# Turning the expert loop of a diffusion trunk layer: gate and up of slot s+1 ahead of down of slot s

## The reference

```python
gates = jnp.sum(jax.nn.one_hot(ids, N_EXPERTS, dtype=jnp.float32) * w_e[..., None], axis=-2).astype(h.dtype)
y = jnp.zeros_like(h)
for e in range(N_EXPERTS):
    hid = jax.nn.silu(h @ wg[e]) * (h @ wu[e])
    y = y + gates[..., e:e + 1] * (hid @ wd[e])
```

## Time and profile before

| | us |
|---|---|
| median of 3 runs | 1084.62 (1083.42 to 1086.98) |
| profiled execution | 1086.46 |
| its span, first to last instruction | 1084.7 |
| PE matmul busy | 900.0 (83%) |
| DVE busy | 718.8 (66%) |
| ACT busy | 415.1 (38%) |
| POOL busy | 392.1 (36%) |
| POOL down remainders (L621), 64 | 186.8 |
| DVE gate/up remainders (L1524), 62 | 156.8 |
| ACT rounding of gate/up (L1134), 64 | 119.5 |

### The profile page before, as it was taken

The page is one execution under the profiler, slowest core; times in us unless marked ns, Lnnn a source line. Parts: engine busy times, 40 slices in busy tenths (PEclk is TensorE's granted clock), DMA queues, the critical chain, the costliest instruction groups (busy, mean ns, idle before and its releaser), DMA issues.

```text
span 1084.7 us, 12383 instructions
## 1 busy us (share of the span) xinstructions
PE 900.0 (83%) x3689; PEld 632.3 (58%) x3690; DVE 718.8 (66%) x794; ACT 415.1 (38%) x520; POOL 392.1 (36%) x181
## 2 busy tenths in 40 slices
PE   6789999949798899992379998999999899988800
PEld 2354444414345478882358886888888677767700
DVE  2234778996883353446885778568646988888648
ACT  1333535325436221113242454435414556556212
POOL 1000735910000000003253647156341777766672
PEclk9989999969899999995589998999999888888955
DMA  8884405015205422316555748476452888887494
GB/s 318 292 330 135 176 20 193 0 39 187 105 0 203 184 78 112 117 78 255 188 190 212 279 168 317 159 271 238 158 223 86 317 317 309 325 311 268 168 358 190
DMA packets 96277, 213.48 MB, mean 197 GB/s; under 512 B 11007, under 2 KB 31613, under 8 KB 96253
## 3 DMA queue, kind: packets, MB, share of 16 engines
q1 hardware_dynamic: 85708, 174.37, 43.9%
q0 software_dynamic: 5904, 21.50, 5.5%
q10 hardware_dynamic: 4640, 17.30, 3.9%
HBM read 180.12 MB, written 33.03 MB: 197 GB/s over the span
## 4 chain that ended last, share of the span: by engine, by line
PE 51%; DVE 28%; issue 8%; DVEq 4%; DMA 3%; ACT 3%; POOL 2%; SPq 0%; ACTq 0%; POOLq 0%
PE bank L701 10%; DVE WP L1524 7%; PE bank L908 3%; PE bank L888 3%; PE bank L887 3%; PE bank L886 3%; PE bank L909 3%; PE bank L910 3%; PE bank L814 3%; PE bank L815 3%; PE bank L816 3%; DVE rkt L1538 2%; PE bank L745 2%; PE bank L683 2%; DVE U L1279 2%
## 5 line engine op out<-in xcount | busy, mean ns | idle before, releaser
L621 POOL TENSOR_TENSOR WP<-raw,WP 128x1024 fp32r<-128x1024 f32 x64 | 186.8, 2947 | 0.7 <-ACT WP L1138 0.5
L701 PE MATMUL bank<-hT,wring 128*128 128x512 f32 x384 | 169.3, 600 | 2.6 <-ACT hT L966 1.9
L1524 DVE TENSOR_TENSOR WP<-raw,WP 128x2048 fp32r<-128x2048 f32 x62 | 156.8, 2568 | 11.7 <-ACT WP L1134 8.3
L1134 ACT ACTIVATE WP<-raw 128x2048 fp32r<-128x2048 f32 x64 | 119.5, 1917 | 90.8 <-issue 84.9
L886 PE MATMUL bank<-WP,xp 128*128 128x512 f32 x368 | 144.1, 391 | 1.5 <-DVE xp L1561 1.5
L888 PE MATMUL bank<-WP,xp 128*128 128x512 f32 x368 | 143.8, 391 | 0.0
L887 PE MATMUL bank<-WP,xp 128*128 128x512 f32 x368 | 143.7, 391 | 0.0
L701 PEld LDWEIGHTS bank<-hT,wring 128*128 128x128 f32 x384 | 73.7, 193 | 93.5 <-issue 90.0
L617 POOL TENSOR_TENSOR held<-held 128x1 f32<-128x1 f32 x24 | 36.2, 1508 | 218.7 <-DVE idg L1553 210.8
L633 POOL TENSOR_TENSOR WP<-raw,WP 128x2048 fp32r<-128x2048 f32 x2 | 9.0, 4532 | 283.6 <-ACT WP L1134 283.6
L908 PE MATMUL bank<-WP,hp 128*128 128x512 f32 x184 | 83.2, 452 | 0.0
(11 more groups left out here) (278 smaller groups left out, 1503.6 us busy)
## 6 DMA issues: line engine op xcount, KB each, us to landing
raw<-in_expert_w_gate SPq DMA_DIRECT2D x64, 512.0 KB, 3.9
raw<-in_expert_w_up SPq DMA_DIRECT2D x64, 512.0 KB, 6.4
raw<-in_expert_w_down SPq DMA_DIRECT2D x64, 512.0 KB, 8.1
mring<-in_mod_w SPq DMA_DIRECT2D x20, 1024.0 KB, 5.3
expert_rows<-ysc ACTq DMA_DIRECT2D x23, 512.0 KB, 7.0
expert_rows<-g SPq DMA_DIRECT2D x16, 512.0 KB, 11.4
wring<-in_w_in SPq DMA_DIRECT2D x12, 512.0 KB, 6.0
mslot<-in_mod_w SPq DMA_DIRECT2D x4, 1024.0 KB, 14.9
```

Of the source, the lines that this page charges most:

```text
L621: pool.tensor_tensor(WP[:, j, 1, 2 * D:], raw[:, j, 2 * D:], WP[:, j, 0, 2 * D:].bitcast(F32), ALU.subtract).then_inc(s_lod[j], 1)
L701: mm = pe.matmul(o_, wring[:, n % 3, k, :], src, start=k == 0, stop=k == KD - 1)
L1134: A_(WP[:, j, 0, 0:2 * D], raw[:, j, 0:2 * D], ACT.Copy).then_inc(s_hgu, 1)
L1524: tt(WP[:, j, 1, 0:2 * D], raw[:, j, 0:2 * D], WP[:, j, 0, 0:2 * D].bitcast(F32), ALU.subtract).then_inc(s_logu[j], 1)
```

## The change

Only the expert loop and what surrounds it change.

- PE: the loop runs W-1 times. Turn q does gate and up of slot q+1, rows of q+2, numbers of q+3, down of q, hidden transposes of q+1. Gate and up of slot 0 with its transposes stand before the loop, down of the last slot after it. All four hidden transposes go to bank 7 and are released together.
- DVE: three gate/up remainders (not one) come ahead of the hidden product, the fourth after the row numbers; the scaling of slot q stands between that and the hidden remainder of q+1. Gate/up work goes by the flag of slot q+1. `gcol` has a column for every slot.
- ACT: three roundings of gate/up ahead of the tanh, then tanh, rows, the fourth rounding, the down roundings (by the flag of slot q), the hidden copy, the store of y.
- POOL: the gather is one slot further ahead; the down remainders go by the flag of q.
- SP: the load order is gate/up of e+1, then down of e.
- The last slot's y is scaled into `xg` and stored under a semaphore of its own. `tab` has one column more. The zeroing of start-up buffers counts on one semaphore.

```diff
-TAB = MAXT + 3
+TAB = MAXT + 4
...
-            with sp.Fori(1, NE) as e:
-                for j in range(KE):
-                    sp.wait_ge(s_logu[j], e)
-                    load_gate_up(bass.ds(e, 1), j)
-                for j in range(KE):
-                    sp.wait_ge(s_lod[j], e)
-                    load_down(bass.ds(e, 1), j)
+            next_gate_up(1, 1)
+            next_down(1, 1)
+            next_gate_up(2, 2)
+            with sp.Fori(2, NE - 1) as e:
+                next_gate_up(e + 1, bass.ds(e + 1, 1))
+                next_down(e, bass.ds(e, 1))
+            next_down(NE - 1, NE - 1)
...
+            pool.wait_ge(s_xgt, 4)
+            gather(2)
             with pool.Fori(0, MAXT // 2) as it:
                 for par in range(2):
-                    with pool.If(2 * it + par < W):
...
+                    with pool.If(2 * it + par + 1 < W):
+                        q = 2 * it + par
+                        L = pool.value_load(tab[0:1, 2, bass.ds(q, 1)], min_val=0, max_val=1)
+                        E = pool.value_load(tab[0:1, 0, bass.ds(q + 1, 1)], min_val=0, max_val=NE - 1)
+                        pool.wait_ge(s_xgt, 2 * q + 6)
+                        gather(q + 3)
                         with pool.If(L > 0):
                             for j in range(KE):
-                                split_down(E1, j)
+                                split_down(E, j)
...
-                        pe.wait_ge(s_xgr, 2 * s + 2)
-                        gate_up(E, par, 0)
-                        gate_up(E, par, 1)
-                        gate_up(E, par, 2)
-                        gate_up(E, par, 3)
-                        turn_rows(s + 1, 0)
-                        turn_rows(s + 1, 1)
-                        turn_hidden(s, 0)
-                        turn_hidden(s, 1)
-                        slot_numbers(s + 2, E2)
+                        pe.wait_ge(s_xgr, 2 * q + 4)
                         for j in range(KE):
-                            down(s, E, j)
+                            gate_up(E1, 1 - par, j)
+                        turn_rows(q + 2, 0)
+                        turn_rows(q + 2, 1)
+                        slot_numbers(q + 3, E3)
+                        for j in range(KE):
+                            down(q, E0, j)
+                        turn_hidden(q + 1)
+            for j in range(KE):
+                down(W - 1, NE - 1, j)
...
+                        with act.If(L1 > 0):
+                            early_hi(q + 1, E2)
+                        tanh_and_rows(q + 1, par)
+                        with act.If(L1 > 0):
+                            late_hi(q + 1, E2)
+                        with act.If(L0 > 0):
                             for j in range(KE):
-                                act.wait_ge(s_dd, 4 * s + j + 1)
+                                act.wait_ge(s_dd, 4 * q + j + 1)
                                 hi_down(E1, j)
-                        act.wait_ge(s_ye, 2 * s + 4)
-                        act.dma_start(y_d[bass.ds(s, 1)].rearrange("a p d -> (a p) d"),
+                        hidden_hi(q + 1)
+                        act.wait_ge(s_ye, 2 * q + 4)
+                        act.dma_start(y_d[bass.ds(q, 1)].rearrange("a p d -> (a p) d"),
...
+                        with dve.If(L1 > 0):
+                            for j in range(KE - 1):
+                                lo_gate_up(E2, j)
+                        hidden(q + 1)
                         for r in range(2):
-                            lo_rows(s + 1, 1 - par, r)
-                        slot_ids(s + 2)
-                        with dve.If(L > 0):
-                            for j in range(1, KE):
-                                lo_gate_up(E1, j)
-                        dve.wait_ge(s_dd, 4 * s + 4)
+                            lo_rows(q + 2, par, r)
+                        slot_ids(q + 3)
+                        with dve.If(L1 > 0):
+                            lo_gate_up(E2, KE - 1)
                         dve.wait_ge(s_ys[par], 16 * it + 16)
...
+                        scale_y(q, ysc[:, par])
+                        hidden_lo(q + 1)
+                        slot_gates(q + 3)
+                        E4 = dve.value_load(tab[0:1, 0, bass.ds(q + 4, 1)], min_val=0, max_val=NE - 1)
+                        T4 = dve.value_load(tab[0:1, 1, bass.ds(q + 4, 1)], min_val=0, max_val=TAB - 1)
+                        prepare_slots(q + 4, E4, T4)
+            dve.wait_ge(s_xg, 16 * W + 32)
+            scale_y(W - 1, xg[:])
```

More of the change, by code:

```diff
@@ L626, in gather @@
                 if not isinstance(q, int):
-                    hold(q - 2)
+                    hold(q - 3)
                 pool.indirect_dma_start(out=xg[:], out_offset=None, in_=xn_d,
@@ L1154, in _, with early_hi, late_hi, tanh_and_rows @@
             W = act.value_load(tab[0:1, 3, 0:1], min_val=NE, max_val=MAXT)
+            def early_hi(s, E1):
+                for j in range(KE - 1):
+                    act.wait_ge(s_gud, 4 * s + j + 1)
+                    hi_gate_up(E1, j)
+            def late_hi(s, E1):
+                act.wait_ge(s_gud, 4 * s + 4)
+                hi_gate_up(E1, KE - 1)
+            def tanh_and_rows(s, nxt):
+                act.wait_ge(s_gate, s + 1)
+                A_(sg[:], bank[0][:], ACT.Tanh, scale=0.5).then_inc(s_sg, 1)
+                for r in range(2):
+                    hi_rows(s + 1, nxt, r)
@@ new lines, in hidden_hi @@
+            def hidden_hi(s):
+                act.wait_ge(s_hT, s + 1)
+                A_(hp[:, 0], bank[7][:].rearrange("p (k n) -> p k n", n=P), ACT.Copy).then_inc(s_hfr, 1)
+            L0 = act.value_load(tab[0:1, 2, 0:1], min_val=0, max_val=1)
+            E1 = act.value_load(tab[0:1, 0, 1:2], min_val=0, max_val=NE - 1)
+            with act.If(L0 > 0):
+                early_hi(0, E1)
+            tanh_and_rows(0, 1)
+            with act.If(L0 > 0):
+                late_hi(0, E1)
+            hidden_hi(0)
@@ L1572, in _ @@
             slot_ids(1)
-            slot_gates(1, 1)
+            slot_gates(1)
             for r in range(2):
@@ L1589, in _, with hidden @@
             W = dve.value_load(tab[0:1, 3, 0:1], min_val=NE, max_val=MAXT)
+            def hidden(s):
+                dve.wait_ge(s_sg, s + 1)
+                stt(out=sg[:], in0=sg[:], scalar=1.0, in1=bank[0][:], op0=ALU.add,
+                    op1=ALU.mult).then_inc(s_sil2, 1)
+                dve.wait_ge(s_sil2, s + 1)
+                dve.wait_ge(s_gud, 4 * s + 4)
+                for h in range(2):
+                    hs = slice(h * 2 * P, (h + 1) * 2 * P)
+                    tt(sg[:, hs], bank[1][:, hs], sg[:, hs], ALU.mult).then_inc(s_hid, 1)
@@ new lines, in scale_y, with hidden_lo @@
+            def scale_y(s, to):
+                dve.wait_ge(s_dd, 4 * s + 4)
+                for h in range(2):
+                    hs = slice(h * HALF, (h + 1) * HALF)
+                    stt(out=to[:, hs], in0=bank[4 + h][:], scalar=gcol[:, bass.ds(s, 1)], in1=g5[:, hs],
+                        op0=ALU.mult, op1=ALU.mult).then_inc(s_ye, 1)
+            def hidden_lo(s):
+                dve.wait_ge(s_hfr, s + 1)
+                tt(hp[:, 1], bank[7][:].rearrange("p (k n) -> p k n", n=P), hp[:, 0].bitcast(F32),
+                   ALU.subtract).then_inc(s_hps, 1)
@@ new lines, in _ @@
+            L0 = dve.value_load(tab[0:1, 2, 0:1], min_val=0, max_val=1)
+            E1 = dve.value_load(tab[0:1, 0, 1:2], min_val=0, max_val=NE - 1)
+            with dve.If(L0 > 0):
+                for j in range(KE - 1):
+                    lo_gate_up(E1, j)
+            hidden(0)
+            for r in range(2):
+                lo_rows(1, 1, r)
+            slot_ids(2)
+            with dve.If(L0 > 0):
+                lo_gate_up(E1, KE - 1)
+            hidden_lo(0)
+            slot_gates(2)
```

144 lines of the change are left out of this document (61 added, 83 removed).

## The result

After: 1092.92 us, median of 8 runs (1089.61 to 1096.41). Before, in runs taken beside it: 1086.1 (1083.42 to 1088.42). The ratio is 1.0063, with a 95% interval of 1.0042 to 1.0083, so the change makes the kernel slower, by about 6.8 us (0.6%). The forecast was 1080.0, with a range of 1066 to 1090; both the sign and the range missed it. The profiled execution of after took 1091.68, its span is 1089.9 against 1084.7.

A forecast was written before the change was run, and what follows sets the result against it. PE was taken to bound shared turns (18.9 us), DVE plus what POOL takes from it being the second limit. The terms summed to -5.0 us, 1079.6 on the 1084.62 median, stated as 1080, range 1066 to 1090.

The forecast's parts named there:

- (a): Prologue: two more DVE remainders delay the first hidden transposes by 4.5 us; the first turn takes 0.8 us more.
- (b): Turns of shared experts: no waits; three turns before slot 4's end save 0.5 us, eight later turns 1.5 us.
- (c): Two turns around slot 5: the collision falls in a turn with slack; 23.6 + 21.4 becomes 37.7, saving 7.3 us.
- (d): Single-slot turns, slots 15 to 22: first -4.8 us, second -3.8, five more +1.6 in all, at 24.1 each.
- (e): The end: last turn +2.2 us, transposes to the end of down +3.8, scaling and storing the last result 0.
- the 20.5 us worked out from a bandwidth of 358 GB/s: Single-slot turns: estimated transfer time of 7.4 MB of weights, which would add 1.6 us to each of two turns.
- (f): Parts taken at 0: load order, ACT's order, POOL's wait for rows, PE's extra table read, table column, start-up waits.
- The upper bound of 16.5 us: PE's one extra table entry a turn: 0.75 us times 22 if exposed; taken as 0.
- The sign named in the prediction: Turns of shared experts: waits there, or single turns at 22.7 or below, would show the prediction wrong.
- the 4.48 us row: A DVE gate/up remainder before the hidden product in the kernel before, 2.29 us alone, delayed beside POOL's down remainders.
- first rival: Single turns: splits meet PSUM operations and issue gaps, five turns fall to 22.7; 1073 us, or 1057; chance 0.2.
- the load order alone moves nothing: SP's queue: the new order of weight loads by itself has no effect, since SP mostly waits for releases.

The follow-up runs named there:

- the prologue run: Kernel after with one gate/up remainder instead of three ahead of the first hidden product, the other two after the row numbers: 1089.01 us, ratio 1.0017.
- The run with the reads first: Kernel after with PE's three table entries read ahead of the hidden transposes instead of behind them: 1085.99 us, ratio 0.9989.
- the splits paced: Kernel after with table reads first and one prologue remainder, plus POOL waiting for each down split's end before issuing the next: 1067.42 us, ratio 0.9799.
- the fastest kernels: Kernel after with table reads first, one prologue remainder, one early and three late remainders in the loop: 1052.09 us; with POOL also waiting between splits: 1053.77 us.
- the short loops: Loops of PE, ACT, DVE and POOL cut from 32 to 24 slots: 1092.68 us on the kernel after, 1087.06 us on the kernel before.

## Why the prediction was wrong

By its own steps, in the two profiled executions. The differences add up to +5.7 us, the spans differ by +5.2.

| step | forecast | measured |
|---|---|---|
| (a) first hidden transposes | +4.5 | +4.0 |
| (a) first turn | +0.8 | 21.2 to 23.3: +2.1 |
| (b) three turns to slot 4's end | -0.5 | 57.1 to 56.15: -0.9 |
| (c) slot 5, two turns | -7.3 | 45.0 to 42.5: -2.5 |
| (b) eight turns after it | -1.5 | 152.4 to 148.4: -4.0 |
| (d) first single turn | -4.8 | 23.6 to 18.4: -5.2 |
| (d) second | -3.8 | 23.8 to 22.85: -1.0 |
| (d) five more | +1.6 | 118.9 to 124.1: +5.2 |
| (e) last turn | +2.2 | 20.3 to 22.7: +2.3 |
| (e) transposes to the end of down | +3.8 | 7.3 to 9.4: +2.1 |
| (e) end of down to the stored result | 0 | 5.3 to 8.9: +3.6 |

*What held.* The reading of what bounds the kernel: PE in shared turns, DVE and the port in single ones. (a), by the prologue run: 4 to 5 us, and 20.7 against 25.2 us in its trace. (b) was better than forecast, since I took 18.86 for PE's floor; by the reading above, 0.8 of it were the numbers' matmuls behind a wait that passed late, which the earlier trace rows alone do not show. The first single turn is covered, 18.4 where I had 18.9; the 20.5 us worked out from a bandwidth of 358 GB/s did not hold it back (against my 18.9 and 20.0 they would have added 1.6 and 0.5 us, not 1.6 twice). Of the last turn the size is right.

*The step that failed first is (f), at nothing.* I put the extra table read under 5 us of queued matmuls, and argued from shared turns of the kernel before, which show no idle PE there. But in that kernel, 24 matmuls of down stand between the transposes' wait and the next table reads. In the new order the wait stands directly ahead of them, so all three reads are exposed each time the product is late, not one more read of 0.75 us. The upper bound of 16.5 us was named and then not used. The run with the reads first gives 7 us back, about what the change cost. In the table it stands in the first turn, in slot 5 (gaps of 1.8 and 0.4 us) and hidden in (b), where the gains would have been larger. The sign named in the prediction, waits in turns of shared experts, is there.

*Step (d) had the right mechanism and the wrong split of the loss.* The forecast has the splits start 5.1 us after the transposes; they start at 902.82, 5.0 after them. It has four instructions of DVE lose 0.1, 2.4, 2.4 and 2.3 us in turn, 7.2; one lost all 8.6. That is 1.4 us more a turn, of which the rest of the sum gives 0.7 back (16.2 where I had 16.9): 24.8 against 24.1. The failed step is the sentence that the 4.48 us row shows POOL's waiting split to go first. In the earlier trace rows the two alternate, but there a split had itself been made to wait by a remainder. The trace of the kernel before held the other case too, near its end, where POOL's four additions are queued and none of them is blocked at first:

```profile
1054.68 9.23 POOL L670 TENSOR_TENSOR fa<-fa,fb 128x1024 f32<-128x1024 f32 x4
```

```profile
1057.07 7.93 DVE L1641 TENSOR_TENSOR fx<-fx,fa 128x1024 f32<-128x1024 f32 x1 [3.21 <-POOL fa L670]
```

DVE's addition, 1.22 us alone, begins with the second of the four and ends 1.1 us after the last. I had not read these rows for this.

In the second single turn (22.85 where I had 20.0) the same hold stood: DVE is busy for 22.1 us of it, where I had let the ranks and the table pass in between. Step (c) failed by it too: in its second turn L1580 takes 8.78 us (664.76), and PE waits 1.15 us for the one-hot table. With the reads mended the two turns still take 41.2 us, with the splits paced 36.7, where I had 37.7. (c) and (d) together miss by 10.8 us (4.8, -0.4, 2.8 and 3.6), as much as the whole table (10.7); they are the larger part of the failure.

*Step (e).* Last down was less dear, since PE was at its full clock. But "scaled and stored as before: 0" was wrong by 3.6 us: DVE goes through the empty passes of its loop first. Without them 1.9 us come back in the trace, and the store meets a load that used to be over. Both come from where the loops end, which I had not followed past the last down.

*What I did not price at all.* The regrouping of the remainders, three ahead of the product instead of one, went into (d) as a part of the new order. It is a change of its own, and by itself costs 35 us. The turned loop makes room for three of them ahead of the product, and with splits of POOL to come that room was better left empty. The forecast came near to it in its first rival (splits that meet PSUM operations and gaps, 1057 to 1073), but took it as chance and not as an order that can be written. Likewise the load order: "the load order alone moves nothing" does not hold inside the new order, where the old one costs 57 to 61 us. Nothing of after's time is traced to it. The new load order was not run on the kernel before, nor the old one with the single early remainder, so what it is worth without the regrouping is open.

*What stays open.* Why the port alternates in one case and stays with POOL in the other is described by the runs (queued splits without a gap; 0.16 us between them; a split that had to wait first) and not explained. What sets the single turns of the fastest kernels, POOL or the transfers, was not separated. The end of the kernel was only read, apart from the short loops.

## What to carry to other kernels

Turning a loop and reordering the work inside it are two changes: price and run them apart, since here the turned loop gains 2.8% with DVE's old order (0.9722) and loses 0.6% with the new one. When an instruction is moved, look at what the sequencer of its engine does next to it: scalar reads behind a wait are free only while matmuls are queued ahead of them, wherever the next late wait is. And where two engines share a port, lay the work that needs no port beside the other's run, or put a small wait between its instructions where they would run unbroken; one tiny instruction at the wrong place cost 8.8 us a turn.

## What was not expected of the hardware

A subtraction of 128 x 8 elements on DVE, 0.2 us alone, stood for 8.8 us behind four POOL instructions of 2.4 us that had been queued without a gap, and a remainder of 2.3 us for 11.5. With 0.16 us between the four, no instruction of DVE lost more than one split. The Trainium skill, "SBUF — State Buffer", section "SBUF: two separate sides", says that whichever instruction starts first has the pair for the whole instruction. The rows agree for one instruction (4.48 = 2.3 + 2.2); that the loser waits for a whole queue of them is more than it says. By the records an earlier start does not protect from it either: near the end of after, DVE's L1715, 1.28 us alone, starts at 1058.36, ahead of four additions of POOL (1058.73 to 1067.96), and takes 10.70.

Three table reads and a branch on PE behind a wait took 2.5 us from the start of the transposes (602.61 to 605.09), of which 0.6 are the transposes. The eight matmuls of the numbers take 0.34 us when queued ahead and 1.07 behind a wait that passes late. POOL's indirect gather (L637) takes 0.97 us beside PSUM operations and 2.85 beside remainders.
